# Layer 1's attention scores computed as three rounded products in a two-layer mixer kernel

## The reference, cut to what matters

```python
s_loc = jnp.einsum("bnqkgd,bnskd->bnkgqs", qb, kb, preferred_element_type=jnp.float32) * scale
s_ctx = jnp.einsum("bnqkgd,bskd->bnkgqs", qb, k_ctx, preferred_element_type=jnp.float32) * scale
s_loc = jnp.where(valid[None, :, None, None], s_loc, -jnp.inf)
p = sink_softmax(jnp.concatenate([s_loc, s_ctx], axis=-1), sink_b)
...
out = jnp.einsum("bnkgqs,bnskd->bnqkgd", p_loc, vb) + jnp.einsum("bnkgqs,bskd->bnqkgd", p_ctx, v_ctx)
```

## Time and profile before

| | |
|---|---|
| median of 3 runs | 1270.64 us (1268.4 to 1271.11) |
| the profiled execution, its own time | 1269.71 us |
| span of its trace | 1267.9 us |
| PE busy | 1223.3 us, 96% of the span |
| DVE busy | 796.6 us, 63% |
| ACT busy | 544.3 us, 43% |
| granted PE clock, mean | 0.994 of full speed |
| layer 1's scores, in the trace | 1016.2 to 1106.0 us, four groups |

### The profile page before, as it was taken

The page is one execution under the profiler, slowest core; times in us unless marked ns, Lnnn a source line. Parts: engine busy times, 40 slices in busy tenths (PEclk is TensorE's granted clock), DMA queues, the critical chain, the costliest instruction groups (busy, mean ns, idle before and its releaser), DMA issues.

```text
span 1267.9 us, 16907 instructions
## 1 busy us (share of the span) xinstructions
PE 1223.3 (96%) x6838; PEld 975.4 (77%) x6838; DVE 796.6 (63%) x1251; ACT 544.3 (43%) x856; POOL 9.7 (1%) x11
## 2 busy tenths in 40 slices
PE   2999999999999999999999999999999999999995
PEld 1555776667777777776778888989888988889995
DVE  5334646766656677673366555696889977646554
ACT  5222445442224434454342222354765445575542
POOL 0000100000000000000100000000000000000000
PEclk9899999999999999999999999999999999999998
DMA  9999655556754344332347656443422634325542
GB/s 335 350 348 348 222 214 226 199 199 227 276 215 162 141 170 171 133 118 115 133 183 244 214 212 214 145 149 122 162 85 93 216 136 146 133 92 194 181 167 67
DMA packets 80878, 236.36 MB, mean 186 GB/s; under 512 B 9376, under 2 KB 54176, under 8 KB 59424
## 3 DMA queue, kind: packets, MB, share of 16 engines
q1 hardware_dynamic: 80800, 235.27, 52.4%
HBM read 230.54 MB, written 2.10 MB: 183 GB/s over the span
## 4 chain that ended last, share of the span: by engine, by line
PE 91%; ACT 3%; DVE 2%; SPq 2%; DMA 1%; issue 1%; DVEq 0%; ACTq 0%
PE psum_block L787 22%; PE psum_block L788 21%; PE psum_block L789 21%; PE psum_ada L627 4%; PE psum_ada L664 2%; PE psum_scores L814 2%; PE psum_scores L715 1%; SPq L576 1%; PE psum_scores L717 1%; PE psum_scores L716 1%; PE psum_scores L851 1%; PE psum_scores L884 1%; PE psum_scores L864 1%; DMA bd<-in_w_ada 1%; PE psum_block L911 1%; PE psum_misc L911 1%
## 5 line engine op out<-in xcount | busy, mean ns | idle before, releaser
L787 PE MATMUL psum_block<-h_hi,w_hi 128*128 128x256 f32 (+1 forms) x1648 | 561.9, 341 | 3.4 <-DVE h_lo L1332 1.7
L788 PE MATMUL psum_block<-h_lo,w_hi 128*128 128x256 f32 (+1 forms) x1648 | 553.4, 336 | 0.0
L789 PE MATMUL psum_block<-h_hi,w_lo 128*128 128x256 f32 (+1 forms) x1648 | 553.2, 336 | 0.0
L1340 DVE TENSOR_TENSOR w_lo<-raw,w_hi 128x1024 fp32r<-128x1024 f32 x210 | 255.3, 1224 | 335.8 <-ACT w_hi L1004 335.6
L1004 ACT ACTIVATE w_hi<-raw 128x1024 fp32r<-128x1024 f32 x210 | 220.9, 1059 | 465.5 <-PE psum_block L789 426.4
L787 PEld LDWEIGHTS psum_block<-h_hi,w_hi 128*128 128x128 f32 x1648 | 312.6, 190 | 65.2 <-issue 28.2
L788 PEld LDWEIGHTS psum_block<-h_lo,w_hi 128*128 128x128 f32 x1648 | 312.9, 190 | 32.8 <-issue 1.9
L789 PEld LDWEIGHTS psum_block<-h_hi,w_lo 128*128 128x128 f32 x1648 | 312.8, 190 | 32.7
L1609 DVE SCALAR_TENSOR_TENSOR Y<-glu,small,Y 128x512 f32<-128x512 f32 (+1 forms) x240 | 130.4, 614 | 0.0
L1158 ACT ACTIVATE T<-psum_scores,stats 128x512 f32<-128x512 f32 (+1 forms) x48 | 29.0, 617 | 46.5 <-DVE stats L1657 46.5
L627 PE MATMUL psum_ada<-raw,cstat 128*32 128x512 f32 x384 | 47.8, 600 | 0.0
(11 more groups left out here) (210 smaller groups left out, 1192.2 us busy)
## 6 DMA issues: line engine op xcount, KB each, us to landing
raw<-in_w_blocks SPq DMA_DIRECT2D x105, 1024.0 KB, 4.9
raw<-in_w_ada SPq DMA_DIRECT2D x81, 1024.0 KB, 6.8
qreg<-in_w_blocks SPq DMA_DIRECT2D x8, 896.0 KB, 11.7
glu<-in_w_ada SPq DMA_DIRECT2D x5, 1024.0 KB, 11.8
kv<-in_w_ada SPq DMA_DIRECT2D x5, 1024.0 KB, 12.0
bd<-in_w_ada SPq DMA_DIRECT2D x5, 1024.0 KB, 11.9
Y<-in_xT SPq DMA_DIRECT2D x8, 512.0 KB, 8.6
T<-in_xT SPq DMA_DIRECT2D x16, 256.0 KB, 5.2
```

The costliest lines, as they stand in the source:

```text
L787: mm(ps[:, cols], hi, hh[:, k, t], start=(at == 0), stop=False)
L788: mm(ps[:, cols], hi, hl[:, k, t], start=False, stop=False)
L789: last = mm(ps[:, cols], lo, hh[:, k, t], start=False, stop=(at == DT - 1))
L1340: V.tensor_tensor(wl[:, u % 4, 0:n], raw_of(item)[:, cols], wh[:, u % 4, 0:n].bitcast(F32), ALU.subtract).then_inc(*C.up("lo", u))
```

## The change

Layer 1's scores are now made as in layer 0: three rounded products per head instead of one plain fp32 product. The value products of layer 1 stay plain fp32. Therefore the tuple SPLIT becomes two, SPLIT for scores and SPLIT_PV for values; in layer 1 only the keys are split (`split_kv` with one part, at step 19), and each group's queries are split to T[0] and T[1] (Q_AT), which hold the probabilities of the group before until their transposes are done; so ACT's `split_q` waits for the last transpose of the group before, not for its value products.

```diff
-KV_SPLIT = 18
-SPLIT = (0,)
+KV_SPLIT = [18, 19]
+SPLIT, SPLIT_PV = (0, 1), (0,)
+Q_AT = [4, 0]
...
-                        q_hi, q_lo = (TR[:, 4 + i, g * QB:(g + 1) * QB] for i in range(2))
+                        q_hi, q_lo = (TR[:, Q_AT[l] + i, g * QB:(g + 1) * QB] for i in range(2))
...
-                if l in SPLIT:
+                if l in SPLIT_PV:
                     pe.wait_ge(*C.at("p_lo", l, s, GROUP - 1))
...
-                for part in range(2):
+                for part in range(2 if l in SPLIT_PV else 1):
...
-                    act.wait_ge(*C.at("pv", l, max(x for x in groups(l) if x < s)))
+                    last = max(x for x in groups(l) if x < s)
+                    act.wait_ge(*(C.at("pv", l, last) if l in SPLIT_PV else C.at("p_tp", l, last, GROUP - 1)))
...
-                fn(TR[:, 4, :].rearrange("p (g t) -> p g t", g=GROUP), q_group(l, s), ACT.Copy).then_inc(*C.up("q_hi", l, s))
+                fn(TR[:, Q_AT[l], :].rearrange("p (g t) -> p g t", g=GROUP), q_group(l, s), ACT.Copy).then_inc(*C.up("q_hi", l, s))
...
-                if b == KV_SPLIT and l in SPLIT:
+                if b == KV_SPLIT[l] and l in SPLIT:
                     split_kv(l)
...
-                V.tensor_tensor(TR[:, 5, :].rearrange("p (g t) -> p g t", g=GROUP), q_group(l, s),
-                                TR[:, 4, :].rearrange("p (g t) -> p g t", g=GROUP).bitcast(F32), ALU.subtract).then_inc(*C.up("q_lo", l, s))
+                V.tensor_tensor(TR[:, Q_AT[l] + 1, :].rearrange("p (g t) -> p g t", g=GROUP), q_group(l, s),
+                                TR[:, Q_AT[l], :].rearrange("p (g t) -> p g t", g=GROUP).bitcast(F32), ALU.subtract).then_inc(*C.up("q_lo", l, s))
...
-                if b - TP_LAG[l] in groups(l) and l in SPLIT:
+                if b - TP_LAG[l] in groups(l) and l in SPLIT_PV:
                     p_lo(l, b - TP_LAG[l])
```

More of the change, by code:

```diff
@@ L1195, in att_pT @@
                     act.wait_ge(*C.at("p_tp", l, s, g))
-                    fn((TR if l in SPLIT else T)[:, 4 + k0:8, g * QB:(g + 1) * QB],
+                    fn((TR if l in SPLIT_PV else T)[:, 4 + k0:8, g * QB:(g + 1) * QB],
                        psS[:, g, k0 * P:TOK].rearrange("p (k q) -> p k q", q=P), ACT.Copy).then_inc(*C.up("pT", l, s, g))
```

## The result

The changed kernel takes 1273.22 us (median of 9 runs, 1271.81 to 1275.13), beside 1270.6 us for the kernel before on the same chip (9 runs). The ratio is 1.0026, with a 95% interval of 1.0016 to 1.0036: **slower by about 3 us**. Run again later, beside 22 runs of the kernel before, it came out at 1.0022 (1.0013 to 1.0031).

The account below looks back on a forecast made before the run. PE, busy 96% of the span, was taken to bound the kernel; 5.6 us of waits less 2.5 saved gave +3.1 us. From the middle of the profiled and median bases this meant 1273.3 us, range 1270.4 to 1277.0.

Parts of the forecast that it names:

- What PE saves: Layer 1's scores: three rounded products save PE 0.63 us per group, 2.52 us over four groups, at least 2.2.
- a whole rounded product less per head: Rival on layer 1's scores: saving 0.23 us for each of 16 heads, 3.7 us, giving 1272.1 us; chance 0.05.
- ACT adds nothing: ACT's copies of keys at step 19 and of each group's queries fall in gaps or finish in time, costing nothing.
- Group 22: First score product waits 2.27 us for q_lo on DVE, whose list kv_lo pushes back.
- Group 25: First score product waits 0.5 us for q_lo, which follows att_out on DVE.
- Group 29: First score product waits 2.5 us for q_lo, behind six taps, a rotary turn and a w_lo on DVE.
- Group 32: q_lo ends by 1100.75, before PE is ready at 1102.13, so the scores don't wait.
- Uncovered weight loads: Each of three PE waits uncovers a weight load of 0 to 0.19 us; 0.1 taken, 0.3 us together.
- What is late next: After the scores, PE's 1.4 us wait before value products and 0.7 us after pointwise products stay, taking up no delay.
- absorbed: Rival: PE's later waits of 1.4 and 0.7 us shrink, up to 2.1 us back, giving 1271.2 us; chance 0.12.
- The clock: Rival: one long PE wait halves the clock, 3.4 us lost, 1276.7 us, or 1280 for both; chance 0.11.
- The sum: Whole kernel: 5.6 us of waits less 2.5 saved gives +3.1 us, bounds +2.4 and +3.8.

Follow-up runs that it names:

- PE's part alone: Kernel before with three rounded products per layer 1 head on ready stand-in operands, no splits or waits for them: ratio 0.998, stage 2.63 us shorter.
- run with the longer wait: Changed kernel with q_lo of group 29 computed four times in a row: ratio 1.0075 to the kernel before.
- busy waits: Ten overwritten products on PE inside the waits of groups 22 and 29: changed kernel 1.0022, with keys split at step 18 1.0012, against the kernel before.

## Why the prediction was right

It said 1273.3 us, slower, with 1270.4 to 1277.0; measured were 1273.22 us. The mechanism and its terms held, as the steps below show. That the two figures lie within 0.1 us is partly luck: the executions of the changed kernel spread over 3.3 us, and the forecast started from a middle chosen between two bases 0.93 us apart. Its steps:

- **What PE saves.** 2.52 us forecast, 2.43 measured in the trace, which includes the uncovered weight loads, and 2.63 with PE's part alone. Taking the price of a head from layer 0's rows, and not a whole rounded product less per head, was the right choice.
- **ACT adds nothing.** Right; the copies ended before DVE came to need them, and no wait for them is in the traces.
- **Group 22.** 2.27 us forecast, 2.18 measured; the other traces with the keys at step 19 gave 1.97 to 2.55 us. The forecast's chain on DVE began at a wait for a DMA at step 18, and this is what varies. DVE, run with the longer wait, kernel after and run with the taps moved:

```profile
996.22 0.42 DVE L1544 TENSOR_TENSOR lnr<-lnr,small 128x256 f32<-128x256 f32 x1 [0.92 <-DMA lnr<-qreg]
997.90 0.43 DVE L1544 TENSOR_TENSOR lnr<-lnr,small 128x256 f32<-128x256 f32 x1 [1.10 <-DMA lnr<-qreg]
998.92 0.43 DVE L1544 TENSOR_TENSOR lnr<-lnr,small 128x256 f32<-128x256 f32 x1 [1.51 <-DMA lnr<-qreg]
```

  Counted from the start of the stage these are 15.48, 15.69 and 16.08 us, and PE's waits were 1.97, 2.18 and 2.55 us: in all six traces with the keys at step 19 (and no busy waits) the difference is 13.51 to 13.53 us. So a later DMA lengthens PE's wait by as much. The share of kv_lo was put at 0.96 us; moving it to step 18, where it fills that wait for the DMA, gave 1.37 us in both traces, 0.81 less than 2.18.
- **Group 25.** 0.5 us forecast, 0.56 us more measured. What I had not seen is that PE already stood still there for 0.29 us in the kernel before: the last projection product starts at 1042.37 and the first score product at 1042.78, where 0.12 us would do (PE's timeline, kernel before). PE's list has it wait for att_out, which ended at 1042.64; no row of the waits tells it.

```profile
1042.37 0.28 PE L789 MATMUL psum_block<-h_hi,w_lo 128*128 128x256 f32 x1
```

  I wrote that nothing PE waits for at the scores was late; for this group that was wrong, and since I took PE's start from the score product itself, it left the sum alone.
- **Group 29.** 2.5 us forecast, 2.57 measured, and 2.56 or 2.57 in each of the six traces with idle waits that left DVE's list there as it was. **Group 32.** None, none.
- **Uncovered weight loads.** 0.1 us per wait forecast; the scores behind a wait took 3.25 us against 3.19 without, so 0.06 us per wait.
- **What is late next.** Right: PE's waits of 1.4 and 0.7 us stayed as they were in every variant, so the delay was not absorbed.
- **The clock.** In the changed kernel's own traces it did not fall, as the forecast's case had it. The rival was nearer than its chance of 0.11 says: three of the eight traces with an idle wait of 2.4 us or more show it, though neither of the changed kernel's own, each time behind group 29's wait, for 1.56 to 1.57 us rather than the 3.4 I had worked out from the opening.
- **The sum.** +3.1 us forecast for the profiled execution; the stage gave +2.84 and the ratio 3.3 us, in the repeat 2.8.

Two things told above were off. The waits were said to show as rows for DVE's q_lo; two of the three appear under "issue", and only the timeline tells what they wait for. And the blocks of a layer are numbered 0 to 55, not 0 to 43.

## What to carry to other kernels

When an operand has to be prepared by another engine, price the change by where the preparing instruction lands in that engine's list, not by that engine's busy share: at 63% busy DVE still worked for 21 us (997.90 to 1018.92) without waiting for anyone ahead of group 22's scores. Put the new instruction ahead of work that nobody waits for, and move such work to steps where the engine waits anyway. When a wait is taken away, look at the reader's next wait for the same engine, since a part of the gain can come back there, as 1.3 us did when only the queries moved.

## What the runs showed of the hardware

The clock of TensorE can fall behind a single wait in the midst of dense work. Behind group 29's wait of 2.56 to 2.57 us it stayed at full level (2.4 GHz) in four traces and went to half (1.2 GHz) in two, and it went to half in the one trace where that wait was 4.74 us. Behind group 22's waits, 1.97 to 2.55 us in six traces, it never fell, nor behind the waits of 1.4 us before the value products; so the length of the wait alone doesn't tell, and what decides is open. The fall begins 0.2 to 0.9 us after the engine has taken up work again, so the products behind the wait are slow and the wait itself isn't longer. It lasts 3.4 us, and each one cost 1.56 to 1.57 us. A plain fp32 product of 512 columns with a mask product takes 0.97 us, three rounded ones with the mask 0.81 and four 1.04.
